# A two-layer trunk on one core: the last two experts joined by a one-hot product, the round flag read earlier, values of eight heads computed late

## What is computed

```
for l in range(DEPTH):
    proj = rms_norm(x, attn_norm[l]) @ w_in[l]        # q, k, v of 6 "a", 5 "b", 5 "c" heads
    oa = diff_attention(...)                          # a: two softmaxes, the second subtracted
    ob = stick_breaking_attention(...)                # b: log-sigmoids summed from the right
    oc = forgetting_attention(...)                    # c: softmax with a summed forget bias
    x = x + concatenate([oa, ob, oc]) @ w_out[l]      # each head RMS-normed before
    x = x + moe_ffn(rms_norm(x, ffn_norm[l]), ...)    # sum over the token's two experts of
                                                      # gate * (silu(t @ wg[e]) * (t @ wu[e])) @ wd[e]
```

## Time and profile before

| | |
|---|---|
| median of 3 runs | 2129.95 us |
| the profiled execution, its span | 2122.7 us, 2121.0 us |
| granted TensorE clock, mean | 0.954 |
| busy: TensorE, VectorE, ScalarE | 1884.9, 1597.2, 1436.7 us |

### The profile page before, as it was taken

How to read it: one execution, slowest core, us unless ns; L and a number is a source line. 1 busy time by engine, 2 the same in 40 slices (tenths; PEclk the granted TensorE clock), 3 DMA queues, 4 the chain that set the end, 5 groups by cost and what they waited for, 6 DMA issues and landing times.

```text
span 2121.0 us, 31136 instructions
## 1 busy us (share of the span) xinstructions
PE 1884.9 (89%) x8974; PEld 1484.9 (70%) x8974; DVE 1597.2 (75%) x2301; ACT 1436.7 (68%) x2278; POOL 92.2 (4%) x86
## 2 busy tenths in 40 slices
PE   7999998995999999999489999989869999999993
PEld 6877776784677777677377777767757777677772
DVE  5567676546999999999464676665579999999993
ACT  5555555433888988989355555654448988988982
POOL 0000000001000000000000000000010000000000
PEclk9999999996999999999789999999879999999996
DMA  6434343454999999999534344435569999999993
GB/s 259 159 139 158 142 158 119 175 203 151 394 398 405 402 400 413 396 408 407 230 141 141 138 159 152 153 115 188 189 210 407 404 403 404 402 406 397 405 381 138
DMA packets 83005, 575.14 MB, mean 271 GB/s; under 512 B 11760, under 2 KB 12016, under 8 KB 13264
## 3 DMA queue, kind: packets, MB, share of 16 engines
q1 hardware_dynamic: 75600, 542.01, 66.0%
q0 software_dynamic: 7296, 31.85, 4.3%
HBM read 567.52 MB, written 23.07 MB: 278 GB/s over the span
## 4 chain that ended last, share of the span: by engine, by line
PE 64%; ACT 11%; issue 11%; DVE 9%; DMA 3%; ACTq 1%; DVEq 0%; POOLq 0%; POOL 0%; SPq 0%
PE bank L775 9%; PE bank L777 9%; PE bank L776 9%; PE bank L940 6%; ACT wh L522 6%; PE bank L924 6%; PE bank L942 6%; PE bank L941 6%; PE bank L926 5%; DVE wl L1091 3%; PE bank L907 2%; ACT rows L719 2%; PE bank L915 1%; DMA proj<-picks 1%; ACT wT L706 1%
## 5 line engine op out<-in xcount | busy, mean ns | idle before, releaser
L1091 DVE TENSOR_TENSOR wl<-raw,wh 128x1024 fp32r<-128x1024 f32 x640 | 767.7, 1222 | 325.8 <-ACT wh L522 324.9
L522 ACT ACTIVATE wh<-raw 128x1024 fp32r<-128x1024 f32 x640 | 664.3, 1054 | 407.4 <-PE bank L777 341.0
L1091 DVE TENSOR_TENSOR wl<-proj,wh 128x1024 fp32r<-128x1024 f32 x384 | 455.3, 1221 | 46.6 <-ACT wh L522 46.1
L924 PE MATMUL bank<-wh,xh 128*128 128x512 f32 x1024 | 428.0, 418 | 32.4 <-DVE wl L1091 29.4
L522 ACT ACTIVATE wh<-proj 128x1024 fp32r<-128x1024 f32 x384 | 394.5, 1052 | 66.5 <-PE bank L942 50.1
L775 PE MATMUL bank<-wh,xh 128*128 128x512 f32 x1024 | 418.8, 409 | 5.8 <-DVE xl L1128 3.1
L926 PE MATMUL bank<-wl,xh 128*128 128x512 f32 x1024 | 405.9, 396 | 0.0
L777 PE MATMUL bank<-wh,xl 128*128 128x512 f32 x1024 | 404.2, 395 | 0.0
L776 PE MATMUL bank<-wl,xh 128*128 128x512 f32 x1024 | 403.7, 394 | 0.0
L924 PEld LDWEIGHTS bank<-wh,xh 128*128 128x128 f32 x1024 | 194.3, 190 | 120.2 <-DVE wl L1091 80.6
L775 PEld LDWEIGHTS bank<-wh,xh 128*128 128x128 f32 x1024 | 195.8, 191 | 49.1 <-DVE wl L1091 9.5
(11 more groups left out here) (209 smaller groups left out, 1539.0 us busy)
## 6 DMA issues: line engine op xcount, KB each, us to landing
raw<-in_expert_units SPq DMA_DIRECT2D x192, 1024.0 KB, 9.2
proj<-in_expert_units SPq DMA_DIRECT2D x192, 1024.0 KB, 9.4
raw<-in_in_units SPq DMA_DIRECT2D x96, 1024.0 KB, 4.8
raw<-in_out_units SPq DMA_DIRECT2D x32, 1024.0 KB, 4.8
proj<-picks POOLq DMA_DIRECT2D x8, 1024.0 KB, 8.1
expert_rows<-rows POOLq DMA_DIRECT2D x4, 1024.0 KB, 4.3
x<-in_x SPq DMA_DIRECT2D x2, 1024.0 KB, 6.4
wide<-in_norms POOLq DMA_DIRECT2D x2, 1024.0 KB, 5.3
```

What stands on the lines that cost most here:

```text
L522: act_(wh[:, h % CUT, :], ring[j][:, h % 2 * HALF:(h % 2 + 1) * HALF], ACT.Copy)\
L924: mm(bank[m][:, :], stacked[b][:, 2 * h + c, :], wh[:, j, k], start=(h + c == 0), stop=False)
L1091: v.tensor_tensor(wl[:, h % CUT, :], ring[(first + h // 2) % slots][:, h % 2 * HALF:(h % 2 + 1) * HALF], wh[:, h % CUT, :].bitcast(F32), A ...
```

## The change

It has five parts. (1) Experts 14 and 15 are no longer scattered: their results stand above each other in rows (64 rows each), and TensorE multiplies them by a one-hot matrix back (slots x tokens, built once in the first step) into PSUM, four times 512 columns for two token tiles, in f32; VectorE adds that to x. (2) GpSimd reads the other 14 experts' rows back from picks earlier, in the closing phase, once the last weight unit has landed, and SyncE starts the next layer's weights only when these have landed. A row that no expert wrote is masked by in_round, and so that it holds a number, each layer begins with a fill of picks from x_in, DRAM to DRAM, 2 x 2 MiB. (3) The flag is read ahead of the closing phase (decide). (4) The gains of the next layer are copied while the router runs. (5) In attention eight heads have v late (LATE = 8), TURN is changed, a stick-breaking head's MIDDLE and all behind it come one half later, and the products with v of heads 8 to 15 come at halves 89 to 97.

```diff
-LATE = NH - 4
+LATE = NH - 8
-TURN = dict(zip((19, 23, 27, 31, 36, 43, 51, 55, 59, 67, 75, 79, 83, 86, 90, 92), range(NH)))
+TURN = dict(zip((19, 23, 28, 31, 36, 43, 51, 55, 60, 63, 67, 71, 75, 78, 84, 87), range(NH)))
+LATE_OUTPUT = (89, 90, 91, 92, 96, 96, 97, 97)
-MIDDLE = steps_at(5)
+MIDDLE = steps_at({"a": 5, "b": 6, "c": 5})
...
-MIXED = {91: 0, 92: 1, 93: 2, 94: 3, 97: 4, 98: 5, 100: 6, 101: 7}
+MIXED = {91: (0,), 92: (1,), 93: (2,), 94: (3,), 97: (4,), 98: (5,), 100: (6, 7)}
+JOIN_BANK = (0, 6, 0, 2)
...
+    def decide(self):
+        e = self.e
+        e.wait_ge(self.sems["again_ready"], self.due("again_ready"))
+        self.fence()
+        e.reg_mov(self.go, e.value_load(self.again, min_val=0, max_val=1))
...
-        picked = [spare[:, k * D:(k + 1) * D] for k in range(2 * NT)]
+        picked = [spare[:, 4 * D:5 * D], spare[:, 5 * D:6 * D], rows[:, 1, :], wide[:, :]]
+        last_rows = rows[SLOTS:STACK, 0, :]
+        back = xl[:, 0, :]
...
+                    t_.decide()
+                    e.wait_ge(S["picks_landed1"], t_.due("picks_landed1", 16 * NT))
...
+                e.wait_ge(S["x_landed"], 16 * NT)
+                for k in range(2):
+                    e.dma_start(picks_dram[k * SEQ:(k + 1) * SEQ, :], x_in).then_inc(S["picks_filled"], 16)
...
-                        if k >= 2:
+                        if 2 <= k < LAST + 2:
                             scatter(k - 2)
-                    freed(NE - 1)
-                for k in range(2 * NT):
-                    e.dma_start(picked[k], picks_dram[k * P:(k + 1) * P, :])\
-                        .then_inc(S[f"picks_landed{k // NT}"], 16)
+                    t_.decide()
+                    e.wait_ge(S[f"raw_landed{DEEP - 1}"],
+                              t_.due(f"raw_landed{DEEP - 1}", 16 * NE * EXP_UNITS // DEEP))
+                    for k in range(2 * NT):
+                        e.dma_start(picked[k], picks_dram[k * P:(k + 1) * P, :])\
+                            .then_inc(S[f"picks_landed{k // NT}"], 16)
...
+                def last_store(k):
+                    act_(last_rows[:, k * COLS:(k + 1) * COLS], bank[2 + k][SLOTS:STACK, :], ACT.Copy,
+                         scale=last_weight[SLOTS:STACK, 2:3]).then_inc(S["last_out"], 1)
...
                 at_least("o_ready", i if i < LATE else i - 1)
+                if i >= LATE:
+                    at_least("neg_max", HA + HC)
+                    at_least("z_ready", HB)
...
+            def join():
+                for j in range(4):
+                    e.wait_ge(S["last_out"], t_.due("last_out"))
+                    if j == 2:
+                        e.wait_ge(S["x_cols"], t_.ahead("x_cols", 1) + 4)
+                    for t in range(NT):
+                        last = mm(bank[JOIN_BANK[j] + t][:, :], back[:, t * P:(t + 1) * P].bitcast(F32),
+                                  rows[:, 0, j * COLS:(j + 1) * COLS], start=True, stop=True)
+                    last.then_inc(S["joined"], 1)
...
+                def last_tables():
+                    v.tensor_copy(back, bank[4][:, P:P + SEQ])
...
+                def add_picks(k):
+                    e.wait_ge(S[f"picks_landed{k}"], t_.due(f"picks_landed{k}", 16 * NT))
+                    for t in range(NT):
+                        v.scalar_tensor_tensor(out=x[:, t, :], in0=picked[NT * k + t],
+                                               scalar=in_round[:, k, t:t + 1], in1=x[:, t, :],
+                                               op0=ALU.mult, op1=ALU.add).then_inc(S["dve_done"], 1)
+                def add_last(j):
+                    e.wait_ge(S["joined"], t_.due("joined"))
+                    for t in range(NT):
+                        ins = v.tensor_tensor(x[:, t, c], bank[JOIN_BANK[j] + t][:, :], x[:, t, c], ALU.add)
+                    ins.then_inc(S["x_cols"], 1)
```

More of the change, by code:

```diff
@@ L109, in steps_at @@
         if late is not None and i >= LATE:
-            n = late + i - LATE
+            n = LATE_OUTPUT[i - LATE] + late
         at.setdefault(n, []).append(i)
@@ L387, in trunk @@
             "out_ready out_free proj_free "
-            "act_done dve_done fence").split() + [k for k in FIXED if k not in ("cut_free", "block_out")]}
+            "act_done dve_done fence").split() + [k for k in FIXED if k not in ("cut_free", "block_out", "raw_landed7")]}
         for i in range(DEEP):
@@ L487, in _ @@
                     gather(1)
-                    for k in range(NE + 2):
+                    for k in range(NE + 1):
                         if k < NE:
@@ L952, in list_slots @@
                                   start=(t == 0), stop=(t == NT - 1))
+                if experts[-1] == NE - 1:
+                    pair = [chosen[:, t, LAST:NE, :].rearrange("p n s -> p (n s)") for t in range(NT)]
+                    for t in range(NT):
+                        mm(bank[4][:, 4 * NE:4 * NE + 4], pair[t], info[:, t, NE - 1, :], start=(t == 0),
+                           stop=(t == NT - 1))
+                    for t in range(NT):
+                        last = e.transpose(bank[4][:, (1 + t) * P:(2 + t) * P], pair[t], ident)
                 if experts[-1] in (FIRST - 1, NE - 1):
                     last.then_inc(S["slot_banked"], 1)
+            def join():
[7 more added lines that the diff above has]
+                    last.then_inc(S["joined"], 1)
             def step(b, first=False, last=False):
@@ L1034, in _ @@
                         turn(i)
[L1035 to L1036 removed]
+                    for g in MIXED.get(n, ()):
                         at_least("mix_scaled", g + 1)
@@ L1079, in _ @@
                         down_half(h, h % CUT)
+                    join()
         @block.vector
@@ L1327, in weigh, with out_norms @@
                     ins.then_inc(S["weights_ready"], 1)
-                def out_norms(g):
-                    at_least("o_ready", 2 * g + 2)
-                    k = slice(2 * g, 2 * g + 2)
-                    inverse_root(out_stat, 2 * g, 2 * g + 2, {HD: (2 * g, 2 * g + 2)})
-                    for t in range(NT):
-                        ins = scaled_heads(rows[:, t, 2 * g * HD:(2 * g + 2) * HD], out_stat[:, 2, t, k], 2)
-                    ins.then_inc(S["mix_scaled"], 1)
-                    if g == NH // 2 - 1:
+                def out_norms(first, end):
+                    at_least("o_ready", 2 * end)
+                    inverse_root(out_stat, 2 * first, 2 * end, {HD: (2 * first, 2 * end)})
+                    for g in range(first, end):
+                        k = slice(2 * g, 2 * g + 2)
+                        for t in range(NT):
+                            ins = scaled_heads(rows[:, t, 2 * g * HD:(2 * g + 2) * HD], out_stat[:, 2, t, k], 2)
+                        ins.then_inc(S["mix_scaled"], 1)
+                    if end == NH // 2:
                         e.sem_inc(S["gain_free"], 1)
@@ L1378, in during @@
                             weigh(i)
-                    for g in steps(PAIR, n):
-                        out_norms(g)
+                    if n in PAIR:
+                        out_norms(*PAIR[n])
                     if n > HALVES - 8 and n - HALVES + 7 < 6:
@@ L1497, in _ @@
                 e.wait_ge(S["dve_done"], t_.due("dve_done"))
+                layer_gains(bass.ds((layer + 1) * (2 * NC) + CN["gains"][0], 2 * NC))
                 e.wait_ge(S["rank_banked"], t_.due("rank_banked"))
@@ L1572, in step @@
                             tables(FIRST, NE)
+                            last_tables()
                             ask_again()
```

141 lines of the change are left out of this document (87 added, 54 removed).

## The result

The changed kernel takes 2104.22 us (median of 4, 2098.91 to 2107.85), the kernel before 2130.19 us beside it (4 runs). The ratio is 0.9884 [0.9867, 0.9902]: 26 us faster, where the forecast was 49 us, and 2 us outside its range.

What follows compares the result with a forecast made beforehand. TensorE, busy 1884.9 of 2121.0 us, was taken as the bound, with waits at layer boundary, end and attention. -16.5 - 15.3 + 3 + 3 + 5 - 28 = -48.8 us gave 2081 us, range 2064 to 2102.

Steps and rivals of the forecast that it cites:

- The boundary: Between the layers, last down matmul to layer 2's first half: scatter and picks reading leave the chain, 16.5 us earlier.
- What is left is its branches (3.18 plus some 0.8): Layer boundary, after the last add: VectorE's loop ends cost this, then 1.9 us of rounding, 7 us to the first half.
- T + 15.5: Layer boundary: where the adds end, counted from the last down matmul's end, if pairs 2 and 3 take 3.6 us each.
- T + 19.2: Layer boundary: predicted time of layer 2's first half, in us after the last down matmul's end T; 16.5 us earlier.
- The fill: Start of layer 1: the DRAM to DRAM copy delays the first weights by 5 us; in layer 2 it is covered.
- The end: End of the program: the last add comes earlier, writing out behind it stays 4.1 us; -15.3 us.
- T + 12.4: Boundary and program end: the last add's end, in us after the last down matmul's end, nearer to the full clock.
- Attention: TensorE's waits in attention: 16.8 us go and 3 us of low clock, less new waits; net 14 us a layer.
- For that I take off 2 us: Attention, halves 60 to 87: allowance for VectorE's load as eight heads turn there beside cuts, norms and heads.
- The 3 us a layer that I had booked for the low clock: Attention: low clock behind the waits of 3.98, 7.42 and 3.08 us goes with them, counted as 3 us in all.
- The flag: Ahead of the closing phase: reading the flag early delays ScalarE's first cut, 1.5 us a layer, 3 in all.
- The tables: First expert step: seven more VectorE instructions, two small products and two transposes, 1.5 us a layer, 3 in all.

Runs made afterwards that it cites:

- e1: The changed kernel with the fill of picks issued behind the attention, after the wait for gain_free; 2086.89 us, ratio 0.9793.
- e2: The changed kernel with the expert part run once, without the loop of rounds, fill left in place, flag still read; 2095.21 us, ratio 0.9834.
- e7: The changed kernel with the edits of e1 and e2 together: fill behind the attention, no loop of rounds; 2084.95 us, ratio 0.9786.
- e3: Parts 1 to 4 of the change alone on the kernel before, attention as before; 2115.34 us, ratio 0.994.
- e6: e5 plus three more unused products at the start of each layer, where TensorE waits for rounded x; 2087.01 us, ratio 0.9789.
- e4: Part 5 of the change (the attention tables) alone on the kernel before; 2111.1 us, ratio 0.9907.
- e12: e11 with one head pair's norm moved one half later, behind the weights of the tenth head; 2062.77 us, ratio 0.9691.
- e5: e1 plus nine unused products of 512 f32 columns in TensorE's two waits between router and first expert step; 2086.96 us, ratio 0.9798.
- e8: e1 with the stick-breaking heads' steps moved back to where they were before the change; 2117.92 us, ratio 0.9938.
- e9: e1 with the slot lists of experts 2 to 15 and VectorE's selection moved ahead of the first gathered rows; 2073.32 us, ratio 0.9743.
- e10: e1 with the join's third pair in banks 2 and 3 and its last pair in banks 0 and 1; 2085.21 us, ratio 0.9787.
- e11: e9 and e10 together on the changed kernel; 2067.55 us, ratio 0.9722.

## Why the prediction was too good

The forecast was -48.8 us and the profile shows -23.8. Of the 25 us between them 9.2 are the boundary's, 9.2 attention's, 5.9 the first steps' and 1.4 the start's; the other terms make up the rest. The big cuts came from the mechanism that I had named; what failed were the prices below.

**The boundary (predicted -16.5, measured -7.3).** Failed step: "What is left is its branches (3.18 plus some 0.8)". I had read 3.18 us as the way round the layer loop and took a second loop end for 0.8. Quiet, the second costs 2.9 as well (e1), and beside the fill it costs 8.34. That is 8.34 + 2.88 = 11.2 us instead of 4.0; the join's last two pairs at the low clock add 1.7 (5.40 us against 3.70; part of the way to the worse end that I had named, T + 15.5). The two make 8.9 of the 9.5 us by which the first half is later than T + 19.2.

**The fill (predicted +5, cost 10 to 17).** Layer 1 was sized about right, 6.4 us. The failed step is that in layer 2 I asked only whether weights are covered, which they are; what was hit is VectorE's jump. e1 takes the fill away from both places and is 17 us faster: 5.7 at the start, 5.6 at the boundary, and 6 that stand at no wait and stay open. The same edit between e2 and e7, without the loop of rounds, gives 10.3 us by the medians, 5.4 at the start and 6.5 at the boundary in the profiles. That the fill slows the jump is shown (e1, e2, e7); that it does so by delaying the loading of instructions is my reading of the DMA queues. For 1054 to 1066 us of the changed kernel they are, among others (kind, packets, MB, share):

```profile
q14 instruction: 6, 0.05, 1.4%
q8 instruction: 1, 0.02, 0.7%
```

and for 1059 to 1063 us, when the last data packets of the fill have been started:

```profile
q14 instruction: 4, 0.03, 2.9%
q8 instruction: 1, 0.02, 2.1%
```

So five of the seven packets are moved in these 4 us, behind the fill's, and VectorE goes on at 1062.27. In e1 as many packets on the same queues are moved in the 8 us from 1043 to 1051. Which engine a packet is for the profile does not tell.

The Trainium skill ("Advanced Engine Details and Errata", section "Control Flow Timing") puts a compare-and-branch at some 108 ns, and its section "ISA Cache" says that an engine holds only two lines of instructions. The first is far below the 2.9 and 8.3 us that the traces show here, and the measurement decides; the second fits the instruction packets in the rows above, and no run here tells how many lines an engine holds.

**The end (predicted -15.3, measured -15.0)** and its last add (T + 12.4, measured T + 12.5) were right: no branch, no fill, and the full clock. That it was right to a few tenths is luck in part: in e1, e3 and e6, with the same join, the end takes 19.3 to 19.5 us instead of 17.7.

**Attention (predicted -14 a layer, measured -11.3 and -7.5, -9.8 by e4).** Right in which waits go (but for 1.08 us, which stayed), wrong in the step "For that I take off 2 us" for the eight heads that turn in halves 60 to 87. Two new waits there (2.42 and 1.81), three for norms of 1.2 instead of one, and two for stick weights of 1.9 instead of 1.1 make the sum 15 us and not 10. e12 shows the first to be VectorE's order within one half, worth some 2.4 us a layer. The mean of the two layers followed the waits: 24 to 15 us is 9, and it was 9.4. The single layer does not: in ten profiles with this table and the same waits attention with its router takes 473.6 to 480.1 us. The 3 us a layer that I had booked for the low clock can't be seen against that.

**The flag (predicted +3).** It adds no wait: TensorE's two waits in the closing phase are 2.83 and 1.83 us in the changed kernel, 2.83 and 1.80 before, and e1 and e2 have the flag and take 491.64 to 491.82 us for the other experts, as before. The +1.4 of the changed kernel's profile stands behind these waits, where the clock stays low for longer with TensorE at work (before, then the changed kernel, columns as above):

```profile
1026.00:1031.00 5.00, 5.00 (x19) 4.00 (x18) 1.66 (x2) 2.25 (x3) 0.00 (x0) 0.80 0.26 103
1026.00:1031.00 5.00, 5.00 (x13) 3.86 (x12) 1.23 (x1) 1.22 (x2) 0.00 (x0) 0.50 1.01 424
```

Of the 24 layers profiled with the early flag 11 have it (492.9 to 493.3 us, e5 in both layers), of the four without it none; whether the flag makes it more frequent stays open. That the sum of +2.8 is close to my 3 is luck.

**The tables (predicted +3, profile +8.9).** Mis-sized and not settled. With the tables, and the lists where they were, 18 first steps average 43.2 us (39.22 to 45.32), without them 4 average 40.1 (35.51 to 43.67). So they may cost 3 us a layer, twice what I had taken, but the spread of the step is larger than that, and the 35.51 in the profile of before was the shortest of all with the lists in the step. No run takes the tables alone away.

## What to carry to other kernels

Give each jump at a loop's end a price of its own: here some 3 us on VectorE, and 8 us with a bulk copy running, so no bulk transfer is issued where loops end. When a wait is taken away, name what stood behind it on the same engine and was covered by it; price the next consumer before the gain is booked (e8: 31 us, where one wait of 2.19 a layer was in the sum). Small products between large ones are best put into a wait that is there anyway (e9: 13.6 us).

## What the hardware showed unasked

The granted clock fell from 0.80 to 0.50 while TensorE was busy 5.00 of 5.00 us in every stretch (e5). Executions of one kernel on one chip differ as their clock does: e10 took 2071.6 us at a mean of 0.969 and 2089.67 at 0.960, and 0.009 of 2080 us is 18.7 us, about the whole difference of 18.1. TensorE's waits in attention, on the other hand, agree to 0.1 us between e1, e4, e5, e11 and the changed kernel, so a wait of 2 us can be read from one trace where the time of five runs can't show it.
